# The last two expert positions summed in PSUM instead of through DRAM, with small parameter loads moved from SP to GpSimd

## The chip, the cores and the metric

The kernel runs on one core of a Trainium2 chip. The metric is the device time of one execution in microseconds (us). The engines have separate instruction streams and meet at semaphores: PE (TensorE, matrix products), DVE (VectorE), ACT (ScalarE), POOL (GpSimd) and SP (SyncE, which here only starts transfers). All numbers are float32. Three timed runs of the kernel before gave 972.03, 973.26 and 973.80 us.

## The reference, cut to what matters

Two layers work on 256 latent and 256 context tokens of width 1024. Layer 0 is a mixer of differential attention and mLSTM, layer 1 a two-dimensional Fourier transform with a linear map, and behind each stands the same kind of grouped mixture of experts. After layer 0's mixer only the 256 latent tokens are still needed. For every token a router picks 2 of 16 experts; the layer's own code is

```
y = jnp.zeros_like(h)
for e in range(N_EXPERTS):
    he = jax.nn.silu(h @ w_gate[e]) * (h @ w_up[e])
    y = y + combine[..., e:e + 1] * (he @ w_down[e])
...
x_l = x_l + mod_l[5] * y_l
```

`combine` holds the two shares of a token and is zero elsewhere. `w_gate` and `w_up` are 1024 x 512 and `w_down` is 512 x 1024, so one expert has 6 MB and one layer 96 MB of weights. A `c`-dependent modulation of shift, scale and gate (`silu(c) @ ada_w + ada_b`, 24 column blocks of 512 over both layers) surrounds every sub-layer.

## The kernel before, in words

**Start.** SP loads the inputs and then a stream of 2 MB blocks into six ring slots (`STREAM`, L454): blocks 0 to 3 of the modulation weights (`ada_w`), the key columns of `w_in`, further blocks. Behind the key columns SP also issues the second part of the constants (L463) and seven little loads (L465 to L471: gate columns, convolution taps, router weights and bias, gate bias, sub-norm gain, lambda vectors), and only then the next block of the stream. PE turns blocks 0 to 3 into rows (L1509) and columns (L1518); DVE and ACT modulate the normed input with them (L982, L644); then PE projects the keys (L1578). DVE sums the later modulation blocks itself (`ada0`, L929), eight instructions a block. The first of these is block 4; PE reduces its sum over partitions at L1555 between two projection items.

**Saved modulation sums.** Blocks 12 to 23 belong to layer 1. DVE sums them into the two halves of `bias`, POOL writes each to DRAM (`save`, L562), and DVE may not refill a half until its save has landed. The last block, 23, goes to an area of its own (`third`), which takes that wait away for it.

**Experts.** Positions 0 to 15 of a layer are worked one after another. The tokens of an expert are cut into units of at most 32 rows; a unit's rows were written to DRAM (`unit_rows`) by POOL and are read back by ACT (`load_x`, L793). For a unit PE does `turn_x` (L1786, transpose), `gate_up` (L1809, 64 products), `turn_he` (L1796) and `down` (L1822, 32 products); ACT applies silu (L814); DVE multiplies (`product`, L1366), copies the transposes (L1348, L1354) and scales the result (`result`, L1361). In the usual order PE does `turn_he` of the unit before, `gate_up` of this one, then `down` of the unit before. Weights of three experts fit in SBUF. SP issues an expert's six 1 MB pieces (L485: gate, up, gate, up, down, down) when PE signals that the buffers are free (`expert_begun`, `expert_closed`).

**Results.** DVE puts a result into one of four places of `ys` and ACT stores it with four transfers to DRAM (`unit_results`, L801). When all are stored, POOL fetches with four indirect transfers (`fetch_results`, L584) for each 128-token tile the two result rows of every token, 512 KB each, 2 MB in all. The fetch waits for the landing of the last store. DVE adds them with their shares (`add_fetched`, L1464, four instructions).

**The last position.** Position 15 (`NE - 1`) does not go through DRAM. Its results stay in place 0 of `ys`, and PE multiplies them with a 0-or-share matrix `late_T` straight into banks 0 to 3, which are idle then (`scatter`, L1877). `late_T` is made by DVE from a row of ranks and shares (`late_rows`, 512 columns), which PE makes with one product of `ones` and a table of diagonals (L1891) at position 13; DVE copies it and clears the four banks (`late_row`, L1338 to L1341). At position 15 PE does the `down` of the unit before ahead of `gate_up`. At the end DVE adds the four banks to `xl` (L1457), and the next norm follows. In layer 0 PE also reduces the saved modulation sums of layer 1 (`sum_mod1`, L1924), which SP reads back at L524; four of them stand between the last `down` and the last `scatter`, and they use copies by ACT (L872), which stand behind a wait of ACT for its last row load. `keep_busy` (L1524) are products without use.

## Time and profile before

| | |
|---|---|
| timed runs | 972.03, 973.26, 973.80 us (median 973.26) |
| the profiled execution: its own time | 973.74 us |
| its span, first to last instruction | 971.9 us |
| busy share of the span | PE 83%, weight load 44%, DVE 41%, ACT 18%, POOL 4% |
| the chain that ended last | PE 38%, DMA 26%, DVE 14%, SP's queue 12%, issue 5%, ACT 3% |
| DMA | 320.36 MB, mean 330 GB/s; SP's queue 74.3%, POOL's 5.9%, ACT's 4.8% |
| mean granted TensorE clock | 0.911 of full speed |

The profiled execution is 1.84 us longer than its span, and lies 0.48 us above the median of the timed runs. A busy share is a mean over stages with different limits; the rows below are from single stages. In a timeline the number in brackets is how long the engine had been idle before the row, and what ended that.

### The profile page before, as it was taken

The page shows a single profiled execution, that of the slowest core. Times are in us where ns is not written, and L with a number is a line of the kernel's source. Part 1 is how long each engine was busy: PE and PEld are TensorE (multiplying, and loading weights), DVE is VectorE, ACT ScalarE, POOL GpSimd, SP SyncE. Part 2 cuts the span into 40 slices and gives each one's busy share as a digit, 9 for nine tenths or more (in the row PEclk, how much of TensorE's full clock was granted, in tenths as well). Part 3 has the DMA queues.
Part 4 walks back from the last instruction along what each step waited for, and adds up shares of the span by engine and source line. Part 5 has one row for each costly group of instructions (what it writes and reads, how often), then busy time and mean ns, then how long its engine had stood idle before and what let it go on. Part 6 is the DMA issues. An engine that isn't in the chain of part 4 may idle for free.

```text
span 971.9 us, 18143 instructions
## 1 busy us (share of the span) xinstructions
PE 801.9 (83%) x6954; PEld 432.2 (44%) x6955; DVE 401.4 (41%) x930; ACT 178.0 (18%) x383; POOL 37.9 (4%) x63
## 2 busy tenths in 40 slices
PE   8899989997979685978567986799869979697674
PEld 3544636444554343544234543374335535354332
DVE  3267879867878841211011230433621111112215
ACT  3222010326630111111001110240211110101002
POOL 0000000120000010000000000100010000000010
PEclk9799999999989797999777998799989988899798
DMA  9899977999505987959999999995669899999991
GB/s 342 292 371 348 335 268 269 330 361 314 197 2 216 379 311 277 366 201 414 415 417 415 371 375 413 372 410 227 247 253 412 349 415 415 416 414 416 414 369 56
DMA packets 102104, 320.36 MB, mean 330 GB/s; under 512 B 12704, under 2 KB 27424, under 8 KB 85536
## 3 DMA queue, kind: packets, MB, share of 16 engines
q1 hardware_dynamic: 78448, 282.84, 74.3%
q0 software_dynamic: 4592, 21.54, 5.9%
q10 hardware_dynamic: 19008, 15.22, 4.8%
q8 instruction: 36, 0.59, 0.2%
q14 instruction: 20, 0.16, 0.0%
HBM read 303.71 MB, written 24.25 MB: 337 GB/s over the span
## 4 chain that ended last, share of the span: by engine, by line
PE 38%; DMA 26%; DVE 14%; SPq 12%; issue 5%; ACT 3%; ACTq 2%; POOL 1%; DVEq 0%; POOLq 0%
DMA raw<-in_w_up 12%; DMA arena<-unit_rows 10%; PE bank L1809 8%; SPq L485 8%; PE bank L1588 7%; PE bank L1822 3%; PE bank L1969 3%; PE bank L1524 2%; DVE arena L929 2%; PE bank L1592 2%; PE bank L1597 1%; PE bank L1578 1%; DMA unit_rows<-arena,row_i 1%; SPq L454 1%; SPq L470 1%
## 5 line engine op out<-in xcount | busy, mean ns | idle before, releaser
L1809 PE MATMUL bank<-raw,arena 128*32 128x256 f32 x3392 | 245.7, 428 | 74.2 <-DMA raw<-in_w_up 41.5
L1809 PEld LDWEIGHTS bank<-raw,arena 128*32 128x32 f32 x3392 | 118.5, 120 | 181.1 <-DMA raw<-in_w_up 58.5
L1366 DVE TENSOR_TENSOR arena<-arena,bank 64x256 f32<-64x256 f32 x53 | 22.5, 425 | 339.0 <-ACT arena L814 339.0
L1822 PE MATMUL bank<-raw,arena 128*32 128x256 f32 x1696 | 111.6, 389 | 2.3 <-DVE arena L1354 2.3
L1822 PEld LDWEIGHTS bank<-raw,arena 128*32 128x32 f32 x1696 | 59.6, 113 | 41.4 <-issue 3.7
L1588 PE MATMUL bank<-ring,arena 128*128 128x512 f32 x160 | 69.9, 594 | 0.0
L814 ACT ACTIVATE arena<-bank 64x256 f32<-64x256 f32 x53 | 19.9, 376 | 246.9 <-PE bank L1809 225.5
L1796 PE MATMUL bank<-consts_sb,arena 64*128 64x64 f32 x212 | 36.1, 292 | 32.6 <-DVE arena L1366 21.2
L929 DVE SCALAR_TENSOR_TENSOR bias<-ring,small,bias 128x512 f32<-128x512 f32 x77 | 57.9, 752 | 2.7
L929 DVE SCALAR_TENSOR_TENSOR arena<-ring,small,arena 128x512 f32<-128x512 f32 x63 | 47.4, 752 | 2.2
L1796 PEld LDWEIGHTS bank<-consts_sb,arena 64*128 64x128 f32 x212 | 28.6, 194 | 44.1 <-DVE arena L1366 24.9
L1588 PEld LDWEIGHTS bank<-ring,arena 128*128 128x128 f32 x160 | 30.2, 190 | 37.7 <-issue 37.7
L1524 PE MATMUL bank<-consts_sb 128*128 128x512 f32 x78 | 42.4, 691 | 0.0
L817 ACT COPY arena<-arena 128x256 f32<-128x256 f32 x53 | 21.4, 405 | 113.3 <-DMA arena<-unit_rows 72.3
L814 ACT ACT_TABLE_LOAD x14 | 18.0, 1283 | 95.1 <-issue 95.1
L1361 DVE TENSOR_TENSOR arena<-bank,arena 128x256 f32<-128x256 f32 x49 | 20.8, 425 | 35.1 <-PE bank L1822 34.4
L1578 PE MATMUL bank<-arena,ring 128*128 128x512 f32 x64 | 29.7, 624 | 1.4 <-DVE arena L982 1.4
L1592 PE MATMUL bank<-arena,ring 128*128 128x512 f32 x64 | 29.5, 621 | 0.0
L1730 PE MATMUL bank<-ring,arena 128*128 128x512 f32 x64 | 28.0, 595 | 0.8 <-ACT arena L755 0.8
L1354 DVE COPY arena<-bank 128x128 f32<-128x128 f32 x53 | 15.4, 291 | 29.6 <-PE bank L1796 22.2
L1969 PE MATMUL bank<-ring,arena 128*128 128x512 f32 x64 | 27.6, 592 | 0.0
L659 ACT ACTIVATE arena<-bank 32x256 f32<-32x256 f32 (+2 forms) x30 | 14.3, 476 | 69.5 <-PE bank L1588 45.6
(259 smaller groups left out, 825.3 us busy)
## 6 DMA issues: line engine op xcount, KB each, us to landing
raw<-in_w_gate SPq DMA_DIRECT2D x64, 1024.0 KB, 19.8
raw<-in_w_up SPq DMA_DIRECT2D x64, 1024.0 KB, 21.7
raw<-in_w_down SPq DMA_DIRECT2D x64, 1024.0 KB, 22.7
ring<-in_ada_w SPq DMA_DIRECT2D x24, 2048.0 KB, 13.3
ring<-in_w_in SPq DMA_DIRECT2D x7, 2048.0 KB, 13.5
unit_results<-arena ACTq DMA_DIRECT2D x228, 32.0 KB, 7.2
arena<-unit_rows ACTq DMA_DIRECT2D x55, 128.0 KB, 6.9
ring<-in_w_out SPq DMA_DIRECT2D x2, 2048.0 KB, 42.8
```

Of the source, the lines that this page charges most:

```text
L485: sp.dma_start(dst, src).then_inc(full[s], 16)
L814: nc.scalar.activation(sg[64:P, :], ps[4][0:64, 0:FW], ACT.Silu).then_inc(E["silu_done"], 1)
L929: ins = nc.vector.scalar_tensor_tensor(acc, w[:, k, :], cc[:, k:k + 1], first if k == 0 else acc, ALU.mult, ALU.add)
L1524: mm(ps[bank][:], ident, K_[:, CONSTS["le"][0]:CONSTS["le"][0] + W], start=True, stop=True)
L1578: ins = mm(bank[:], w[:, k, 256 * b + par:256 * (b + 1):2], hT[:, k, :], start=(k == 0), stop=(k == KD - 1))
L1588: ins = mm(bank[:], hT[:, k, t * P:(t + 1) * P], w[:, k, :], start=(k == 0), stop=(k == KD - 1))
L1592: ins = mm(bank[:], w[:, k, a * HD:(a + 1) * HD], hT[:, k, :], start=(k == 0), stop=(k == KD - 1))
L1730: ins = mm(ps[q][:], mgT[:, k, t * P:(t + 1) * P], slot(s)[:, k, :], start=(k == 0), stop=(k == KD - 1))
L1796: ins = mm(ps[6][:, q * 64:(q + 1) * 64], he[64:P, q * P:(q + 1) * P], ident[64:P, 64:P], start=True, stop=True)
L1809: ins = mm(ps[4][o:o + S, 0:FW], xT[:, i, j * S:(j + 1) * S], w[:, k % 4, h * FW:(h + 1) * FW], start=(k == 0), stop=(k == KD - 1))
L1822: ins = mm(ps[5][j * S:(j + 1) * S, 0:XW], hT_e[:, k % QN, k // QN * S:(k // QN + 1) * S], w[:, k % 2, j * XW:(j + 1) * XW], start=(k == 0 ...
L1969: ins = mm(ps[q][:], FT[:, k, t * P:(t + 1) * P], slot(FNET_AT + hf)[:, k, :], start=(k == 0), stop=(k == KD - 1))
```

## The change

Three things change.

- **Two late positions.** `LATE = NE - 2`: positions 14 and 15 are now both summed by `scatter` into banks 0 to 3 and leave out DRAM. PE makes two rows of ranks and shares (into banks 2 and 3), the second kept in the columns of the constants that held the cosine and sine tables. At each of the two positions PE does the `down` of the unit before first, and at position 15 a `scatter` as well, ahead of `gate_up`. The last result that is stored is now position 13's, and `fetch_results` waits for that one. On DVE both `add_fetched` stand in position 15's first unit, ahead of its `product`.
- **Block 23** of the modulation goes through `bias` like the others; the area `third` and SP's waits for the saves are gone.
- **Little loads.** The seven loads are issued by POOL, once PE has used blocks 0 to 2 (`w_used` at 3), and SP goes straight from the constants to the next block.

```diff
@@ the little loads, on SP @@
                 if n == 4:
-                    sp.wait_ge(bias_zero, 2)
                     sp.dma_start(K_[:, K_PARTS[1]:K_PARTS[2]], consts[:, K_PARTS[1]:K_PARTS[2]]
                                  ).then_inc(consts_in, 16)
-                    sp.dma_start(wgt_s.rearrange("p (k n) -> p k n", k=KD),
-                                 w_in_v[:, :, C_G:C_G + NE]).then_inc(smalls_in, 16)
-                    for dst, src in ((convs, convw), (rw_s[:, :, 0:NE], rw.rearrange("(p k) n -> p k n", k=KD)),
...
@@ and on POOL, ahead of its loop over the modulation blocks @@
+            pool.wait_ge(w_used, 3)
+            pool.dma_start(wgt_s.rearrange("p (k n) -> p k n", k=KD),
+                           w_in_v[:, :, C_G:C_G + NE]).then_inc(smalls_in, 16)
...
+            pool.dma_start(lamrow, lamv.to_broadcast([P, 4 * QK])).then_inc(smalls_in, 16)
@@ the fetch, on POOL @@
                 pool.wait_ge(L[l]["y_stored0"], (NE // 2) * 16 * JN)
-                pool.wait_ge(L[l]["y_stored1"], (NE // 2 + 1) * 16 * JN)
+                pool.wait_ge(L[l]["y_stored1"], (NE // 2) * 16 * JN)
@@ ACT, behind position 13 @@
+                n = act.snap(units, min_val=LATE, max_val=MAX_UNITS)
+                store_y(n, n * S, 0)
+                for i in range(LATE, NE):
+                    n_tok = act.value_load(cnt_i[0:1, i:i + 1], min_val=0, max_val=SEQ)
+                    late_unit()
...
@@ DVE, the waits of ada0 @@
-                    if c >= N_ADA + 2 and c < 2 * N_ADA - 1:
+                    if c >= N_ADA + 2:
                         dve.wait_ge(acc_saved[c % 2], 16 * ((c - N_ADA) // 2))
@@ DVE, late_row @@
-                    link(nc.vector.tensor_copy(late_rows, ps[2][:]))
+                    for e in range(2):
+                        link(nc.vector.tensor_copy(late_rows[e], ps[2 + e][:]))
@@ DVE, positions 14 and 15 @@
+                for e in range(2):
...
+                    turn_back(n - 1)
+                    if e == 0:
+                        result(n - 1, 0, NE // 2 - 1)
+                        dve.wait_ge(E["y_stored1"], (NE // 2) * 16 * JN)
+                    else:
+                        late_result(n - 1)
+                        next_weights(1, True)
+                        add_fetched(l, 0)
+                        add_fetched(l, 1)
+                    product(n)
+                    turned(n + 1)
...
                 turn_back(n - 1)
-                add_fetched(l, 0)
                 late_result(n - 1)
-                add_fetched(l, 1)
@@ PE, positions 14 and 15 @@
+                for e in range(2):
+                    ins = mm(ps[2 + e][:], ones, bias[:, e, :], start=True, stop=True)
+                ins.then_inc(late_in_psum, 1)
...
+                for i in range(LATE, NE):
...
+                    turn_he(n - 1)
+                    down(n - 1, prev)
+                    if i > LATE:
+                        scatter(n - 1, False)
+                    gate_up(n, own, True)
+                    turn_x(n + 1, True)
```

PE at the start of position 14 in layer 1, before; `raw_..` are weight pieces, `x8` is eight products of one kind in a row.

```order
L1887 TENSOR_LOAD cnt_i
L1887 ISA x2
L1796 MATMUL bank<-consts_sb,arena 128x64 x2
L1802 REGISTER_ALU
L1809 MATMUL bank<-raw_61,arena 32x256 x2
L1809 MATMUL bank<-raw_62,arena 32x256 x2
```

PE at the same place after the change.

```order
L1904 TENSOR_LOAD cnt_i
L1904 ISA x2
L1804 MATMUL bank<-consts_sb,arena 128x64 x2
L1830 MATMUL bank<-raw_59,arena 32x256 x8
L1830 MATMUL bank<-raw_60,arena 32x256 x8
L1810 REGISTER_ALU
L1817 MATMUL bank<-raw_61,arena 32x256 x2
L1817 MATMUL bank<-raw_62,arena 32x256 x2
```

The `down` of position 13 (L1830, before L1822) stands ahead of position 14's `gate_up` (L1817, before L1809).

DVE at the end of layer 1's experts, before: the last transpose copy, the four adds of fetched rows (L1464) around the last result (L1430), the adds of the four banks (L1457).

```order
L1354 COPY arena<-bank 128x128
L1464 SCALAR_TENSOR_TENSOR xl<-arena,xl 128x1024
L1464 SCALAR_TENSOR_TENSOR xl<-bias,arena,xl 128x1024
L1430 TENSOR_TENSOR arena<-bank,arena 128x256
L1464 SCALAR_TENSOR_TENSOR xl<-arena,xl 128x1024 x2
L1457 TENSOR_TENSOR xl<-xl,bank 128x256 x8
```

DVE after the change, in the first unit of position 15.

```order
L1353 COPY arena<-bank 128x128
L1419 TENSOR_TENSOR arena<-bank,arena 128x256
L1426 COPY arena<-consts_sb 128x1
L1429 ISA
L1316 SCALAR_TENSOR_TENSOR arena<-consts_sb,arena 128x256
L1431 REGISTER_ALU
L1472 SCALAR_TENSOR_TENSOR xl<-arena,xl 128x1024
L1472 SCALAR_TENSOR_TENSOR xl<-bias,arena,xl 128x1024
L1472 SCALAR_TENSOR_TENSOR xl<-arena,xl 128x1024 x2
L1364 REGISTER_ALU
L1365 TENSOR_TENSOR arena<-arena,bank 64x256
```

The four adds (now L1472) have moved from behind the last unit's transpose to a place ahead of the `product` (L1365) of position 15's first unit.

SP in the start stage, before: the constants (L463), the little loads and the next blocks.

```order
L454 DMA ring<-in_w_in 128x8x512
L463 DMA consts_sb<-in_constants 128x1629
L465 DMA small<-in_w_in 128x8x16
L470 DMA small<-in_conv_w 128x24
L470 DMA small<-in_router_w 128x8x16
L470 DMA small<-in_router_b 128x16
L470 DMA small<-in_gate_b 128x16
L470 DMA arena<-in_subln_g 128x128
L471 DMA arena<-in_lam 128x256
L454 DMA ring<-in_ada_w 128x8x512 x4
```

SP after.

```order
L455 DMA ring<-in_w_in 128x8x512
L463 DMA consts_sb<-in_constants 128x1629
L455 DMA ring<-in_ada_w 128x8x512 x4
L455 DMA ring<-in_w_in 128x8x512
L455 DMA ring<-in_ada_w 128x8x512 x3
```

The seven little loads have left SP's queue, and block 4 follows the constants.

## Rows read from the trace of the kernel before

**Rows 1.** Windows: us, busy of PE, PEld, DVE, ACT, POOL, PEclk, DMA share, GB/s.

```profile
932.00:936.00 4.00, 1.11 (x12) 0.15 (x5) 0.00 (x0) 0.00 (x0) 0.00 (x0) 1.00 1.02 408
```

**Rows 2.** Timeline of PE, end of layer 1: start, length, operation [idle before].

```profile
908.10 1.02 PE L1891 MATMUL bank<-bias,consts_sb 128*128 128x512 f32 x2
...
936.11 3.44 PE L1809 MATMUL bank<-raw,arena 128*32 128x256 f32 x28 [2.10 <-DMA raw<-in_w_up]
...
956.89 1.93 PE L1822 MATMUL bank<-raw,arena 128*32 128x256 f32 x32 [0.41 <-DVE arena L1354]
959.94 1.15 PE L1877 MATMUL bank<-arena 32*128 32x256 f32 x16 [1.12 <-DVE arena L1430]
```

**Rows 3.** Timeline of DVE, end of layer 1.

```profile
909.23 0.68 DVE L1338 COPY late_rows<-bank 128x512 f32<-128x512 f32 x1
...
912.97 0.29 DVE L1354 COPY arena<-bank 128x128 f32<-128x128 f32 x1 [0.25 <-issue]
...
940.00 0.42 DVE L1366 TENSOR_TENSOR arena<-arena,bank 64x256 f32<-64x256 f32 x1 [11.66 <-ACT arena L814]
...
962.44 2.73 DVE L1457 TENSOR_TENSOR xl<-xl,bank 128x256 f32<-128x256 f32 x8
```

**Rows 4.** Timeline of ACT, ends of layer 0 and layer 1.

```profile
609.98 0.39 ACTq L793 DMA_DIRECT2D arena<-unit_rows  x1
...
617.08 0.20 ACT L760 ACTIVATE small<-consts_sb 128x1 f32<-128x1 f32 x1 [5.08 <-DMA arena<-unit_rows]
...
929.60 1.78 ACTq L801 DMA_DIRECT2D unit_results<-arena  x4
```

**Rows 5.** Timeline of POOL, the first fetch of each layer.

```profile
611.06 0.98 POOL L584 DMA_INDIRECT arena<-unit_results,row_i  x1 [248.45 <-DMA unit_results<-arena]
...
939.04 0.98 POOL L584 DMA_INDIRECT arena<-unit_results,row_i  x1 [227.70 <-DMA unit_results<-arena]
```

**Rows 6.** DMA queues from 618 to 625 us: packets, MB, share of 16 engines.

```profile
q0 software_dynamic: 403, 1.45, 52.4%
q1 hardware_dynamic: 605, 1.36, 50.9%
```

**Rows 7.** Timeline of DVE, end of layer 0.

```profile
621.08 1.28 DVE L1464 SCALAR_TENSOR_TENSOR xl<-arena,xl 128x1024 f32<-128x1024 f32 x1 [9.45 <-DMA bias<-unit_results,row_i]
...
625.16 2.60 DVE L1464 SCALAR_TENSOR_TENSOR xl<-arena,xl 128x1024 f32<-128x1024 f32 x2 [1.02 <-DMA arena<-unit_results,row_i]
627.98 2.73 DVE L1457 TENSOR_TENSOR xl<-xl,bank 128x256 f32<-128x256 f32 x8 [0.21 <-DVE xl L1464]
```

**Rows 8.** Timeline of PE, end of layer 0.

```profile
617.90 1.96 PE L1924 MATMUL bank<-arena,consts_sb 128*128 128x512 f32 x4 [0.21 <-ACT arena L872]
624.28 2.09 PE L1877 MATMUL bank<-arena 32*128 32x256 f32 x16 [4.42 <-DVE arena L1430]
626.30 3.38 PE L1524 MATMUL bank<-consts_sb 128*128 128x512 f32 x4
...
635.52 3.73 PE L1942 MATMUL bank<-consts_sb,arena 128*128 128x129 f32 x32
```

**Rows 9.** SP's queue in the start stage: the block behind the little loads.

```profile
41.00 12.41 SPq L454 DMA_DIRECT2D ring<-in_ada_w  x4
```

**Rows 10.** Timeline of PE in the start stage.

```profile
32.32 3.33 PE L1509 MATMUL bank<-ring,arena 128*32 128x512 f32 x16 [0.53 <-DMA ring<-in_ada_w]
...
41.80 15.79 PE L1578 MATMUL bank<-arena,ring 128*128 128x512 f32 x32 [1.35 <-DVE arena L982]
58.18 1.12 PE L1555 MATMUL bank<-arena,consts_sb 128*128 128x512 f32 x2 [0.59 <-DVE arena L929]
```

**Rows 11.** Timeline of DVE: modulation blocks 4, 22 and 23, their first instructions.

```profile
51.86 0.75 DVE L929 SCALAR_TENSOR_TENSOR arena<-ring,small,bias 128x512 f32<-128x512 f32 x1 [4.74 <-issue]
...
309.31 0.75 DVE L929 SCALAR_TENSOR_TENSOR bias<-ring,small,consts_sb 128x512 f32<-128x512 f32 x1 [2.65 <-DMA ada_sums<-bias]
...
315.49 0.75 DVE L929 SCALAR_TENSOR_TENSOR arena<-ring,small,consts_sb 128x512 f32<-128x512 f32 x1
```

More of the change, by code:

```diff
@@ L504, in norm_used @@
                     sp.wait_ge(part_ps, l + 1)
-                    for b in range(2):
-                        sp.wait_ge(acc_saved[b], 16 * (N_ADA // 2))
             def stream_used(s):
@@ L1894, in experts @@
[L1894 to L1910 removed]
+                    n = pe.snap(units, min_val=1, max_val=MAX_UNITS)
@@ new lines, in experts @@
+                    turn_he(n - 1)
+                    down(n - 1, prev)
+                    if i > LATE:
+                        scatter(n - 1, False)
+                    gate_up(n, own, True)
+                    turn_x(n + 1, True)
+                    pe.reg_add(units, units, 1)
+                    with pe.If(n_tok > S):
+                        with pe.Fori(S, n_tok, S):
+                            n = pe.snap(units, min_val=1, max_val=MAX_UNITS)
+                            turn_he(n - 1)
+                            gate_up(n, own, False)
+                            down(n - 1, own)
+                            turn_x(n + 1, False)
+                            scatter(n - 1, False)
+                            pe.reg_add(units, units, 1)
```

140 lines of the change are left out of this document (58 added, 82 removed).

## The prediction

> **What bounds the kernel now.** I read the queue table of the page, then windows of 4 us over the end of each layer's experts, then the timelines of PE, DVE, ACT and POOL there, and last the start. At the end of layer 1's experts the transfers set the pace: from 932 to 936 us the 16 DMA engines are fully busy at 408 GB/s, while PE works 1.11 of 4 us [rows 1]. PE's last 28 products of position 15's first `gate_up` begin at 936.11, after 2.10 us of idle time ended by a piece of `up` weights [rows 2]. DVE had been idle for 11.66 us when it does the `product` behind them at 940.00 [rows 3]. What lies between there and the end is a chain of PE and DVE. So two things count: what lands before that last `up` piece, and what DVE does behind the last `down`.
>
> The fetch of results stands in a different place in the two layers. In layer 1 it begins at 939.04 [rows 5], when the last awaited piece has landed, and other work hides it. In layer 0 it begins at 611.06 [rows 5] and is on the path: DVE gets the first tile at 621.08 and the second at 625.16 [rows 7], and the last `scatter` of PE, at 624.28, has waited 4.42 us for DVE [rows 8].
>
> **When the fetch begins after the change.** It now depends on position 13's last result, made by the `down` that comes first at position 14. That `down` needs DVE's transpose copy, at 912.97 [rows 3], which stands behind `late_row`. The second product of `ones` puts 1.02 us before it (length of L1891, [rows 2]) and the second copy 0.68 us [rows 3]: 914.7. The `down` takes 1.93 us at the full clock [rows 2] and up to twice that at the lower level, then 0.42 for the result: stores begin between 917.4 and 919.3. From the stores at 929.60 [rows 4] to the fetch at 939.04 [rows 5] it takes 9.44 us. So the fetch begins between 926.8 and 928.8 instead of 939.04; I take 928. That is 8 us before the last `up` piece lands, inside the stretch where the engines are full.
>
> **Layer 1, the price.** The fetch is 2.1 MB. At 408 GB/s [rows 1] that is 5.1 us, which the weights behind it lose if it goes entirely ahead of them. When both queues had work in layer 0, from 618 to 625, GpSimd's queue moved 1.45 MB and SP's 1.36 MB [rows 6]: equal shares. The other 0.65 MB went in the first 7 us, at less than half of its share. With that slow start the last `up` piece comes about 3.3 us late (0.65 MB owed at 935, paid back at half rate); with equal shares from the start 4.7 to 5.1. Beside it stands DVE: the four adds now come before the `product`. In layer 0 the tiles came 10.0 and 14.1 us after the first issue [rows 5, 7]. From 928 that gives 942.1, and the two adds of the second tile take 2.60 [rows 7]: 944.7. The `product` goes from 940.00 to 944.7, so +4.7 us; bounds 3.3 (only the weights, slow start) and 6.0 (fetch at 928.8 and half a microsecond worse). Position 14's `scatter` (1.15, [rows 2]), the new weights for `late_T`, four more diagonals and the clearing all fall in the 11.66 us of idle time [rows 3] and cost nothing as long as that wait exists. One stored unit less saves 0.13 MB, 0.3 us, which I leave inside the bounds.
>
> The Trainium skill, in "DMA: Bandwidth & Descriptors", section "Queues, rings and completion order", says that every DMA engine goes round the queues that have work and changes at packet boundaries. Rows 6 agree for their 7 us; the first 7 us of that fetch do not. By the rule alone the weights would be 5.1 us late in place of my 4.7 and each layer's `product` 0.4 later.
>
> **Layer 1, the gain at the end.** The last `down` ends at 956.89 + 1.93 = 958.82 [rows 2]. Now the result follows at once (0.42 and some 0.2 of handovers), then the `scatter` (1.15), and the adds of the banks begin at 960.6 instead of 962.44 [rows 3]: −1.8 us. Layer 1 together: +2.9, bounds +1.5 and +4.2.
>
> **Layer 0.** The same order of work shifts position 15's `product` by the same 4.7 us. Then ACT's last load of rows goes from 609.98 to 614.7. It was awaited until 617.08 [rows 4], 7.1 us, so ACT is free at 621.8 for the copies that the second pair of modulation sums needs; that pair goes from 617.90 to 622.6 and ends at 624.6 (1.96, [rows 8]). So the `scatter` starts at 624.6 in place of 624.28: where DVE waited for the fetch, ACT's row load is late next. What is gained is the clock and DVE. Before, PE had idled 4.42 us and the `scatter` took 2.09 [rows 8], against 1.15 at the end of layer 1 [rows 2]: the lower of the two levels, 1.2 GHz against 2.4. Four products behind it took 3.38 [rows 8], so 1.7 at the full clock. Without the idle time this saves up to 0.94 + 1.69 = 2.6 us, and DVE, whose adds begin at 625.8 instead of 627.98 [rows 7], allows 2.2. The first Fourier product (635.52, [rows 8]) comes 2.2 us earlier, or 0.3 later if the clock stays low. I take −1.5, nearer to the full clock; bounds −3.5 (shift of the `product` only 3.3 us) and +1.0.
>
> **The start.** Block 4 was issued at 41.00 [rows 9], behind the seven little loads; now it follows the constants at once. DVE began it at 51.86 [rows 11] and PE waited 0.59 for its sum before 58.18 [rows 10]; a start of the block 0.6 us earlier is enough to take that away: −0.6. PE has no later wait for transfers that this could shorten. Against it, the little loads now run while block 3 is on its way, and PE waits for that block (0.53 idle before 32.32) and from there in one chain to the first projection at 41.80 [rows 10]. POOL may issue them when PE has used block 2, which comes one 2 MB block (5.1 us at the 408 GB/s of [rows 1]) before block 3, so near 28 by estimate; fetched rows needed some us from issue to full share in layer 0 [rows 6], so at most the last 2.4 us before 32.32 are shared equally: 1.2 us, at least nothing. I take +0.5. Together −0.1, bounds −0.6 and +0.6. DVE needs them only behind its part of the modulation, which releases PE at 41.80 [rows 10], so their landing is hardly a risk.
>
> The skill, same page, section "Issuing engines are not separate DMA queues", says that issuing from another engine saves only sequencer time. No row here shows little loads from GpSimd; by the rule block 3 pays for them, as in my +0.5.
>
> **Block 23.** Block 22 began at 309.31 after waiting 2.65 for block 20's save [rows 11]. The save of 21 is one block later, 6.18 us, so it lands at 315.49, just when block 23 starts [rows 11]. 0 to +0.3; I take +0.1.
>
> **Sum.** +2.9 − 1.5 − 0.1 + 0.1 = +1.4 us. On the profiled execution's own 973.74 (span 971.9 and 1.84 around it) that is 975.1. It stands 0.48 above the median of the runs, so I forecast **974.7 us**, +0.15%. This kernel's measurements tell 0.2%, or 1.95 us, from no change, so this counts as no difference.
>
> **Rivals.** *(a) The weights are not held up.* The fetch finds room or is served last. Then layer 1 gains its 1.8; in layer 0 the `scatter` follows the sums at 620.0 in place of 624.28, −4.3, with the clock up to −6.9; the start −0.6. In all −6.7 to −9.3, about 965.3 us. For it: the slow first 7 us in layer 0. Against: 408 GB/s and full engines [rows 1] leave no room. Chance 0.12.
>
> *(b) DVE gets stuck in front of the `product`: slower.* The four adds stand before it, and PE's `turn_he`, all further units and the end stand behind it. This decides as soon as the second tile lands more than about 14 us after the first issue; from there each microsecond costs one in each layer. The weights' queue is deeper here than in layer 0 before. With 2 us more in each: +1.4 + 4.0 = +5.4, 978.7 us. For it: the second tile needed 14.1 us already beside one other queue. Against: the pieces behind the last `up` piece are few. Chance 0.28.
>
> *(c) A milder collision with the clock kept.* Shift 3.3 us in both layers: layer 1 +1.5, layer 0 −3.5, the start −0.6: −2.6, 970.7 us. Chance 0.15.
>
> *(d) The little loads hold up block 3 by more than 1.2 us* or push the constants behind 41.80, which PE also needs: +1 on the forecast, 975.7. Chance 0.05. That the change doesn't do what it says is not in question: the order of instructions shows the moves.
>
> My forecast keeps 0.40, its own range 972.5 to 976.5. The range that should hold 8 in 10 leaves out (a) and the upper part of (b): 970.0 to 978.0. Faster by over 0.2% (below 971.3) holds (a) and most of (c): 0.26. Slower (above 975.2) holds (b), (d) in part and the upper third of the forecast: 0.37. Within: 0.37.
>
> **What would show it.** In layer 1's trace: the fetch near 928 (before 926.8 or after 929 is wrong); the last awaited `up` piece 3.3 to 5 us later; `product` directly behind the fourth add; no add of fetched rows behind the last `down`, 1.8 us between that and the bank adds. In layer 0: the `scatter` near 624.6 and short (1.15). At the start: no wait before L1555's first use, block 3 up to 1.2 us later. If the last `up` piece lands unshifted, the whole of layer 1's price is wrong, and the time is that of (a).

## The result and the profile after

The changed kernel took **985.06 us** (median of 4 runs, 983.35 to 985.42); the kernel before, on the same chip in the same job, 973.53 us (4 runs). The ratio is 1.0112, 95% interval 1.0086 to 1.0137: slower. The forecast of 974.7 us and its range to 978.0 were both wrong. What happened is rival (b), DVE stuck in front of the `product`, at about twice its price (+11.5 us on the medians where it said +5.4). The profiled execution took 985.42 us.

The page of the changed kernel: the span, and PE's and DVE's busy time.

```profile
span 983.6 us, 18211 instructions
...
PE 809.7 (82%) x6990; PEld 436.0 (44%) x6991; DVE 406.1 (41%) x944; ACT 178.1 (18%) x383; POOL 43.0 (4%) x71
```

The span grew by 11.7 us, while the busy shares are what they were or a point less. The loss is waiting. The windows over the end of layer 1's experts show where, with the columns of [rows 1]:

```profile
940.00:944.00 4.00, 0.26 (x2) 0.02 (x1) 0.74 (x1) 0.72 (x2) 0.00 (x0) 0.86 1.02 410
944.00:948.00 4.00, 0.00 (x0) 0.00 (x0) 1.82 (x2) 0.00 (x0) 0.00 (x0) 0.50 0.70 272
948.00:952.00 4.00, 0.41 (x2) 0.41 (x3) 3.42 (x4) 0.00 (x0) 0.00 (x0) 0.50 0.00 0
```

From 940 to 951 PE does nothing, its granted clock falls to half, and at the end the transfers have run dry too: PE waits for DVE, and DVE for the second tile and then for its own two adds. DVE's timeline there answers [rows 3]:

```profile
917.58 0.29 DVE L1353 COPY arena<-bank 128x128 f32<-128x128 f32 x1 [0.23 <-issue]
...
943.25 1.28 DVE L1472 SCALAR_TENSOR_TENSOR xl<-arena,xl 128x1024 f32<-128x1024 f32 x1 [11.34 <-DMA bias<-unit_results,row_i]
...
948.39 2.60 DVE L1472 SCALAR_TENSOR_TENSOR xl<-arena,xl 128x1024 f32<-128x1024 f32 x2 [2.53 <-DMA arena<-unit_results,row_i]
951.12 0.42 DVE L1365 TENSOR_TENSOR arena<-arena,bank 64x256 f32<-64x256 f32 x1
...
974.12 2.73 DVE L1465 TENSOR_TENSOR xl<-xl,bank 128x256 f32<-128x256 f32 x8 [1.34 <-PE bank L1885]
```

The `product` stands right behind the fourth add at 951.12; before it ran at 940.00. Nothing stands any more between the last result and the bank adds but the `scatter`. PE's timeline answers [rows 2]:

```profile
917.92 3.64 PE L1830 MATMUL bank<-raw,arena 128*32 128x256 f32 x32 [4.31 <-DVE arena L1353]
...
937.97 1.92 PE L1817 MATMUL bank<-raw,arena 128*32 128x256 f32 x28 [2.20 <-DMA raw<-in_w_up]
...
951.59 1.11 PE L1804 MATMUL bank<-consts_sb,arena 64*128 64x64 f32 x4 [11.33 <-DVE arena L1365]
952.64 5.54 PE L1817 MATMUL bank<-raw,arena 128*32 128x256 f32 x64
```

The last `up` piece was there at 937.97, only 1.86 us later than before. PE then stood for 11.33 us, and ran the next 64 products at the half clock, 5.54 us; the same 64 take 3.66 in the further unit behind them. ACT's stores of position 13's result and POOL's first fetches of both layers answer [rows 4, 5]:

```profile
922.30 2.48 ACTq L799 DMA_DIRECT2D unit_results<-arena  x4
```

```profile
598.32 0.97 POOL L574 DMA_INDIRECT arena<-unit_results,row_i  x1 [235.60 <-DMA unit_results<-arena]
...
932.41 0.97 POOL L574 DMA_INDIRECT arena<-unit_results,row_i  x1 [218.92 <-DMA unit_results<-arena]
```

The DMA queues while the fetch (GpSimd's queue, q0) and SP's queue (q1) both had work, packets and MB, answer [rows 6]. First the changed kernel from 937 to 943 us, where SP's queue holds weights, then the kernel before from 616 to 622, where it holds the saved sums and constants:

```profile
q1 hardware_dynamic: 329, 1.25, 52.1%
q0 software_dynamic: 325, 1.20, 50.2%
```

```profile
q0 software_dynamic: 424, 1.55, 65.3%
q1 hardware_dynamic: 431, 0.85, 37.6%
```

In both, the two queues moved equal numbers of packets. SP's packets averaged 3.8 KB beside weights and 2.0 KB in the kernel before, the fetch's 3.7 KB in both, so the fetch got 49% of the bytes of the two queues in the first case and 65% in the second.

The end of layer 0, DVE first and PE behind it, answers [rows 7, 8]:

```profile
610.99 1.28 DVE L1472 SCALAR_TENSOR_TENSOR xl<-arena,xl 128x1024 f32<-128x1024 f32 x1 [9.95 <-DMA bias<-unit_results,row_i]
...
616.33 2.60 DVE L1472 SCALAR_TENSOR_TENSOR xl<-arena,xl 128x1024 f32<-128x1024 f32 x2 [2.73 <-DMA arena<-unit_results,row_i]
619.05 0.42 DVE L1365 TENSOR_TENSOR arena<-arena,bank 64x256 f32<-64x256 f32 x1
...
630.06 2.73 DVE L1465 TENSOR_TENSOR xl<-xl,bank 128x256 f32<-128x256 f32 x8 [4.90 <-PE bank L1885]
```

```profile
608.85 3.33 PE L1817 MATMUL bank<-raw,arena 128*32 128x256 f32 x28 [3.19 <-DMA raw<-in_w_up]
...
621.03 3.64 PE L1830 MATMUL bank<-raw,arena 128*32 128x256 f32 x32 [0.38 <-DVE arena L1353]
624.60 4.23 PE L1935 MATMUL bank<-arena,consts_sb 128*128 128x512 f32 x8
628.76 1.15 PE L1885 MATMUL bank<-arena 32*128 32x256 f32 x16
...
637.66 3.73 PE L1953 MATMUL bank<-consts_sb,arena 128*128 128x129 f32 x32
```

The `product` comes at 619.05 (609.36 before), the last `down` behind it at the half clock, and the first Fourier product at 637.66 where it was at 635.52.

**The loss, added up.** POOL wrote layer 1's rows at 708.11, 2.15 us later than before (705.96): that is layer 0 and the start. From there to layer 1's `product` it takes 8.97 us more (951.12 − 708.11 against 940.00 − 705.96). Behind the `product`, 64 + 4 products at the half clock cost 1.88 + 0.45 = 2.33, and the order at the end gives 1.77 back. Together 2.15 + 8.97 + 0.56 = 11.68 of 11.7 us.

### The profile page after: what moved, and what is told of

Its sections match the earlier page's. It is cut to its first block, busy times and chain, and to the rows that moved or that the text cites. A ratio compares the mean times of both kernels' runs of the same rounds, so it can differ in the third digit from the quotient of the medians.

```text
span 983.6 us, 18211 instructions
## 1 busy us (share of the span) xinstructions
PE 809.7 (82%) x6990; PEld 436.0 (44%) x6991; DVE 406.1 (41%) x944; ACT 178.1 (18%) x383; POOL 43.0 (4%) x71
## 4 chain that ended last, share of the span: by engine, by line
PE 45%; DMA 23%; DVE 14%; SPq 8%; issue 5%; ACT 2%; ACTq 2%; POOL 1%; DVEq 0%; POOLq 0%
PE bank L1817 10%; DMA raw<-in_w_up 10%; PE bank L1596 7%; PE bank L1830 6%; DMA arena<-unit_rows 6%; SPq L478 5%; PE bank L1586 3%; PE bank L1980 3%; DMA arena<-unit_results,row_i 3%; PE bank L1600 2%; DMA consts_sb<-in_constants 2%; PE bank L1532 2%; DVE bias L925 2%; PE bank L1804 1%; PE bank L1605 1%
## 5 line engine op out<-in xcount | busy, mean ns | idle before, releaser
L1817 PE MATMUL bank<-raw,arena 128*32 128x256 f32 x3392 | 244.4, 430 | 65.8 <-DMA raw<-in_w_up 36.0
L1817 PEld LDWEIGHTS bank<-raw,arena 128*32 128x32 f32 x3392 | 119.0, 121 | 172.7 <-DMA raw<-in_w_up 51.0
L1365 DVE TENSOR_TENSOR arena<-arena,bank 64x256 f32<-64x256 f32 x53 | 22.5, 425 | 304.8 <-ACT arena L812 299.9
L1830 PE MATMUL bank<-raw,arena 128*32 128x256 f32 x1696 | 114.8, 401 | 10.2 <-DVE arena L1353 10.2
L1830 PEld LDWEIGHTS bank<-raw,arena 128*32 128x32 f32 x1696 | 59.7, 116 | 51.5 <-DVE arena L1353 11.1
L925 DVE SCALAR_TENSOR_TENSOR bias<-ring,small,bias 128x512 f32<-128x512 f32 x84 | 63.2, 752 | 3.0
L925 DVE SCALAR_TENSOR_TENSOR arena<-ring,small,arena 128x512 f32<-128x512 f32 x56 | 42.1, 752 | 2.0
L1532 PE MATMUL bank<-consts_sb 128*128 128x512 f32 x78 | 38.9, 642 | 0.0
L1600 PE MATMUL bank<-arena,ring 128*128 128x512 f32 x64 | 28.5, 605 | 0.0
L1353 DVE COPY arena<-bank 128x128 f32<-128x128 f32 x53 | 15.4, 291 | 28.5 <-PE bank L1804 20.7
```

The source lines that it names most:

```text
L925: ins = nc.vector.scalar_tensor_tensor(acc, w[:, k, :], cc[:, k:k + 1], first if k == 0 else acc, ALU.mult, ALU.add)
L1532: mm(ps[bank][:], ident, K_[:, CONSTS["le"][0]:CONSTS["le"][0] + W], start=True, stop=True)
L1600: ins = mm(bank[:], w[:, k, a * HD:(a + 1) * HD], hT[:, k, :], start=(k == 0), stop=(k == KD - 1))
L1817: ins = mm(ps[4][o:o + S, 0:FW], xT[:, i, j * S:(j + 1) * S], w[:, k % 4, h * FW:(h + 1) * FW], start=(k == 0), stop=(k == KD - 1))
L1830: ins = mm(ps[5][j * S:(j + 1) * S, 0:XW], hT_e[:, k % QN, k // QN * S:(k // QN + 1) * S], w[:, k % 2, j * XW:(j + 1) * XW], start=(k == 0 ...
```

## The experiments

One table serves them all. It gives four stretches of each profiled execution in us: from POOL's first write of rows (L564 of the changed kernel) to the start of the last awaited `up` piece's products, in each layer, then from there to the first Fourier product (layer 0) and to the bank adds (layer 1). What lies between Fourier and layer 1's rows took 70.4 to 70.5 us in all but one (71.5), and what follows the bank adds 9.5 to 9.6. "Early" says where the fetch is released: behind position 13's result (early) or later.

| kernel | fetch | rows to last up, layer 0 | last up to Fourier | rows to last up, layer 1 | last up to bank adds | median us | ratio to before |
|---|---|---|---|---|---|---|---|
| before | late | 249.2 | 28.5 | 230.2 | 26.3 | 973.53 | 1 |
| changed | early | 251.0 | 28.8 | 229.9 | 36.2 | 985.06 | 1.0112 |
| e1 | early | 252.0 | 26.6 | 230.5 | 26.3 | 974.39 | 1.0007 |
| e2 | late | 247.9 | 28.6 | 230.1 | 26.5 | 972.19 | 0.9990 |
| e3 | early | 251.0 | 28.2 | 230.7 | 29.8 | 978.58 | 1.0061 |
| e4 | early | 250.9 | 26.3 | 230.7 | 34.3 | 983.08 | 1.0119 |
| e5 | early | 251.2 | 25.2 | 230.4 | 25.8 | 971.94 | 0.9966 |
| e6 | late | 249.2 | 29.0 | 229.0 | 28.7 | 974.40 | 0.9990 |
| e7 | late | 248.6 | 28.7 | 229.4 | 27.3 | 972.41 | 0.9986 |
| e8 | early | 250.0 | 24.6 | 230.6 | 30.9 | 976.01 | 1.0004 |
| e9 | early | 249.9 | 27.2 | 229.3 | 25.8 | 970.63 | 0.9969 |
| e10 | early | 253.0 | 27.5 | 231.1 | 35.5 | 980.24 | 1.0064 |

The kernel before ran beside each: 973.31 us for e1 to e4, 974.69 for e5 to e8, 973.58 for e9 and e10. Intervals stand with each experiment.

**e1_adds_last: the changed kernel with the adds where they were.**

```diff
@@ changed kernel, DVE, position 15 @@
                         next_weights(1, True)
-                        add_fetched(l, 0)
-                        add_fetched(l, 1)
@@ behind the last copy of transposes @@
                 turn_back(n - 1)
+                add_fetched(l, 0)
                 late_result(n - 1)
+                add_fetched(l, 1)
```

> The kernel after, with the four adds of fetched rows put back behind the last unit's transpose copy (tile 0 before the last result, tile 1 behind it), as the kernel before has them. All else stays: both late positions, down first, the early fetch, block 23, little loads by GpSimd. Theory O (order): DVE waits for the second tile ahead of position 15's product, and that wait is the loss. Then the product of layer 1 comes back from 951.1 to about 942.3 (940.0 plus the 2.2 us by which the stage starts later), PE does not drop to the lower clock there (-2.3), the 1.8 us gained at the end are lost again: -9.5 in layer 1 and -2 to -4 in layer 0, 972 to 975 us. Theory B (bandwidth): the early fetch takes the time from the weights, wherever DVE uses it: 982 us or more.

974.39 us (12 runs), ratio 1.0007, 0.9988 to 1.0025: the whole loss is gone. PE and then DVE at the end of layer 1:

```profile
938.26 3.39 PE L1817 MATMUL bank<-raw,arena 128*32 128x256 f32 x28 [2.98 <-DMA raw<-in_w_up]
```

```profile
942.11 0.42 DVE L1365 TENSOR_TENSOR arena<-arena,bank 64x256 f32<-64x256 f32 x1 [11.59 <-ACT arena L812]
...
961.86 2.60 DVE L1472 SCALAR_TENSOR_TENSOR xl<-arena,xl 128x1024 f32<-128x1024 f32 x2
964.58 2.84 DVE L1465 TENSOR_TENSOR xl<-xl,bank 128x256 f32<-128x256 f32 x8
```

The `product` follows the weights again, although the fetch is as early as in the changed kernel (930.38). So the early fetch, the second late position, the `down` first and the little loads together cost nothing that can be measured; the place of the adds costs it all.

**e2_little_loads: the kernel before with only the little loads moved to POOL.**

```diff
@@ kernel before, SP @@
-                    sp.wait_ge(bias_zero, 2)
...
-                    sp.dma_start(lamrow, lamv.to_broadcast([P, 4 * QK])).then_inc(smalls_in, 16)
@@ POOL, ahead of its loop over the modulation blocks @@
+            pool.wait_ge(w_used, 3)
...
+            pool.dma_start(lamrow, lamv.to_broadcast([P, 4 * QK])).then_inc(smalls_in, 16)
```

> The kernel before with one part of the change alone: the seven little loads issued by GpSimd once PE has used block 2, and SP going straight on. Theory O: this part costs nearly nothing at the end: PE starts the keys up to 1 us late, part of which is made up by a higher clock, 973.3 to 974.8 us. Rival S (start): the little loads and the extra queue cost 3 us or more in all, 976.5 us or more.

972.19 us (12 runs), ratio 0.9990, 0.9973 to 1.0007: no difference, under the 973.3 that was the lower end expected. PE in the start stage:

```profile
42.37 16.27 PE L1578 MATMUL bank<-arena,ring 128*128 128x512 f32 x32 [2.71 <-DMA consts_sb<-in_constants]
58.48 1.02 PE L1555 MATMUL bank<-arena,consts_sb 128*128 128x512 f32 x2
```

The keys now wait for the constants (42.37 against 41.80), and the wait of 0.59 before L1555 is gone, as forecast; L1555 itself comes 0.30 later.

**e3_adds_one_step_later: the adds behind position 15's `product`, ahead of the copy of the transposes.**

```diff
@@ changed kernel, DVE, position 15 @@
-                        add_fetched(l, 0)
-                        add_fetched(l, 1)
                     product(n)
                     turned(n + 1)
+                    if e == 1:
+                        add_fetched(l, 0)
+                        add_fetched(l, 1)
```

> The kernel after, with the four adds one step further down in DVE's stream: behind product and the copy of the next rows in position 15's first unit, still ahead of that unit's transpose copy. Theory O gives a dose: in layer 1 PE can now do the whole second gate_up before it needs DVE, so the wait of DVE for the second tile (until about 951) holds up PE by some 4.5 us instead of 9, and PE hardly drops its clock; in layer 0, with one unit, hardly more than 2 us come back. 975 to 979 us. Theory B: no difference to the kernel after, 983 to 986 us.

978.58 us (7 runs), ratio 1.0061, 1.0041 to 1.0081. DVE in layer 1:

```profile
947.85 2.61 DVE L1473 SCALAR_TENSOR_TENSOR xl<-arena,xl 128x1024 f32<-128x1024 f32 x2 [1.47 <-DMA arena<-unit_results,row_i]
950.82 0.29 DVE L1353 COPY arena<-bank 128x128 f32<-128x128 f32 x1 [0.36 <-DVE xl L1473]
```

The same tile is waited for, but PE has the 64 products of the next unit to do meanwhile and lacks only the copy: half of the loss. Here the wait cost what stood behind it in the order, not what it lasted.

**e4_pe_kept_busy: the changed kernel with 7 (layer 0) and 12 (layer 1) calls of `keep_busy`, of two products each, for PE while DVE waits behind position 15's first `gate_up`.**

```diff
@@ changed kernel, PE, positions 14 and 15, ahead of turn_he @@
+                    if i > LATE:
+                        keep_busy((7, 12)[l], 5)
```

> The kernel after, with products without use (7 in layer 0, 12 in layer 1, into a bank that is free) while PE waits for DVE behind position 15's first gate_up. Theory O counts 11.1 us for DVE's wait in layer 1 and a further 2.3 us because PE restarts at the lower clock (the 64 products behind the wait take 5.5 instead of 3.7 us, the four before them 1.1 instead of 0.66). Then this kernel gets back 2.3 us in layer 1 and 0 to 2 in layer 0: 981 to 983 us. If the lower clock isn't due to the idle time, nothing comes back: 984.5 to 986 us.

983.08 us (4 runs), ratio 1.0119, 1.0084 to 1.0155; by the time it can't be told from the changed kernel, so neither expectation is confirmed by it. The trace shows the clock's share:

```profile
939.62 10.46 PE L1532 MATMUL bank<-consts_sb 128*128 128x512 f32 x24
950.01 0.66 PE L1804 MATMUL bank<-consts_sb,arena 64*128 64x64 f32 x4
950.60 3.66 PE L1817 MATMUL bank<-raw,arena 128*32 128x256 f32 x64
```

With work in the gap the 64 products take 3.66 us and the four 0.66: 2.33 saved behind the wait. The useless products ran 1.8 us past DVE's `product` at 947.78 and ate most of it; in layer 0, where they ended in time, the stretch to Fourier shrank from 28.8 to 26.3. The Trainium skill, "TensorE: Matmul & The Clock Gate", Part 1 on the clock gate, says that the gate sets the array's clock by how busy PE has recently been; these rows agree. Behind the wait the lower clock costs 2.3 us in layer 1 and about as much in layer 0; it is a follow-up cost, not the cause. How long DVE's wait is doesn't set it: the same 64 products took 6.02 us in e10 behind 6.99 us without work, 6.10 in e8 behind 4.21, and 5.25 to 5.6 in e5, e7 and e9 behind 0.31. PE also stands still for the weights before them, and in the kernel before the lower clock fell on the 28 products ahead of the `product` instead (3.44 us, 1.92 in the changed kernel).

**e5_adds_in_idle: tile 0's adds behind position 15's own unit, tile 1's behind its first further unit.**

```diff
@@ e1, DVE, position 15 @@
+                        add_fetched(l, 0)
                         with dve.If(n_tok > S):
+                            further_unit()
+                            add_fetched(l, 1)
...
                 turn_back(n - 1)
-                add_fetched(l, 0)
                 late_result(n - 1)
-                add_fetched(l, 1)
+                with dve.If(n_tok <= S):
+                    add_fetched(l, 1)
```

> The changed kernel with the four adds moved into VectorE's idle time: tile 0's two behind position 15's own unit, tile 1's two behind its first further unit (behind the last product where it has none). Nothing is left out. With the adds behind the last transpose copy, as in e1_adds_last, the bank adds of layer 1 began at 964.58 because the fourth add ended at 964.46, while the product they need could have been scattered at about 961.5. Theory O (the changed kernel lost its time only because VectorE waited for tile 1 ahead of position 15's product; every wait of 3.7 us between two further units holds two adds of 2.6 us for nothing): bank adds about 1.8 us earlier, so 971.8 to 973.4 us. Rival (the adds delay the transposes' copies and with them the down products, or tile 1 is not there when its place comes): 974.5 or more.

971.94 us (12 runs), ratio **0.9966, 0.9947 to 0.9984**: faster than the kernel before. In layer 1 tile 0 was 1.92 us late for its place, which hid behind PE's 64 products. In layer 0 it was there in time, but its adds held the copy for the last `down`, which waited 3.46 us and ran at the half clock (3.64); the stretch to Fourier, which goes over the modulation sums, was 25.2 us all the same. The profiled execution (975.67 us) was the slowest of the twelve and wrote layer 0's first rows 3.5 us later than the kernel before's (361.31 against 357.78); why isn't known.

**e6_fetch_behind_weights: e1, but ScalarE releases the fetch only behind position 15's own unit.**

```diff
@@ e1, ACT @@
-                nc.scalar.copy(s_done[:, l:l + 1], ident[:, 0:1]).then_inc(further_stored, 1)
...
                     late_unit()
+                    if i > LATE:
+                        nc.scalar.copy(s_done[:, l:l + 1], ident[:, 0:1]).then_inc(further_stored, 1)
```

> As e1_adds_last (adds behind the last transpose copy), and the fetch released by ScalarE only behind position 15's own unit, when all weights of the layer have landed. Nothing is left out. Measured so far: from position 14's last `up` piece to position 15's is 5.62 and 5.54 us in the kernel before (layers 0 and 1), 6.73 and 6.08 in e1_adds_last. Theory F (the early fetch holds these weights up): the steps go back to 5.5 to 5.7 us in both layers. Theory P (the down-first order at position 14 frees weight buffers later): the steps stay at 6.1 to 6.7. For the time: layer 1 gains at most 0.5, layer 0 wins 1.2 on the weights and loses about as much on tiles that land at 629, so 973 to 976 us either way; a sum above 978 would say that the fetch's earlier place carries more than I think.

974.40 us (10 runs), ratio 0.9990, 0.9972 to 1.0008, inside what both expected. The step between the last two `up` pieces tells them apart; PE at the end of layer 0:

```profile
601.05 1.92 PE L1818 MATMUL bank<-raw,arena 128*32 128x256 f32 x28 [1.96 <-DMA raw<-in_w_up]
...
606.39 2.43 PE L1818 MATMUL bank<-raw,arena 128*32 128x256 f32 x28 [2.23 <-DMA raw<-in_w_up]
```

5.34 us here and 4.99 in layer 1, against 6.73 and 6.08 in e1 and 5.62 and 5.54 before. In layer 0 theory F holds: this step took 6.1 to 7.2 us in the eight kernels with an early fetch and 5.3 to 5.6 in the four with a late one, and from the rows to the last `up` piece the early ones took 249.9 to 253.0 us, the late ones 247.9 to 249.2. In layer 1 single executions don't settle it: where the rows show the step, it was 5.47 (the changed kernel itself) to 6.08 with an early fetch and 4.99 to 5.60 with a late one.

**e7_before_adds_in_idle: the kernel before with e2's little loads and the adds in the further units' idle time.**

```diff
@@ kernel before, DVE, position 15's further units and the end @@
+                    further_unit()
+                    add_fetched(l, 0)
...
                 turn_back(n - 1)
-                add_fetched(l, 0)
+                with dve.If(n_tok > S):
+                    add_fetched(l, 1)
...
+                with dve.If(n_tok <= S):
+                    add_fetched(l, 0)
                 late_result(n - 1)
-                add_fetched(l, 1)
+                with dve.If(n_tok <= S):
+                    add_fetched(l, 1)
```

> The kernel before with the little loads issued by GpSimd (as e2_little_loads) and, in a layer where the last expert has further units, tile 0's adds behind its first further unit and tile 1's ahead of the last product instead of behind it. Nothing is left out. In the kernel before layer 1's bank adds began at 962.44 behind the fourth add; the products they need were scattered from 959.94 on, which lets them begin at about 961.2. Theory O: 1.2 us less than e2_little_loads (972.2), so 970.4 to 971.6 us, under the kernel before. Rival (tile 0 lands after its place, as tile 1 did in the changed kernel, and holds the copy for the second further unit's down products): no gain or a loss, 972 to 975.

972.41 us (12 runs), ratio 0.9986, 0.9971 to 1.0001: not the 1.2 us less than e2. In its trace the fourth add delays the last result by about half a microsecond, and the 64 products of the first further unit ran at the half clock, 5.6 us. With a late fetch there is one idle place fewer in which a landed tile can be added.

**e8_second_tile_last: the changed kernel with only tile 1's adds moved to the end.**

```diff
@@ changed kernel, DVE @@
                         add_fetched(l, 0)
-                        add_fetched(l, 1)
...
                 late_result(n - 1)
+                add_fetched(l, 1)
```

> The changed kernel with only tile 0's two adds ahead of position 15's product; tile 1's two go behind the last product. Nothing is left out. In the changed kernel tile 0's adds ended at 945.85, tile 1's at 950.99, and the product ran at 951.12. Theory O: the product runs at about 946.1, 5.0 us earlier, PE stands still shorter, and tile 1's adds come back to the end for 0 to 1.8 us: 978.5 to 982 us, between e1_adds_last (974.4) and the changed kernel (985.1). Rival (the price is not the place of the wait but something else that the adds' early place does, such as writes to xl beside the matmuls): 983 or more.

976.01 us (10 runs), ratio 1.0004, 0.9984 to 1.0023: below the range expected. DVE in layer 1, and PE in layer 0:

```profile
936.98 1.28 DVE L1472 SCALAR_TENSOR_TENSOR xl<-arena,xl 128x1024 f32<-128x1024 f32 x1 [9.23 <-DMA bias<-unit_results,row_i]
...
939.71 0.42 DVE L1365 TENSOR_TENSOR arena<-arena,bank 64x256 f32<-64x256 f32 x1
```

```profile
608.08 3.45 PE L1817 MATMUL bank<-raw,arena 128*32 128x256 f32 x28 [3.15 <-DMA raw<-in_w_up]
...
615.04 3.74 PE L1830 MATMUL bank<-raw,arena 128*32 128x256 f32 x32 [0.38 <-DVE arena L1353]
619.97 3.85 PE L1935 MATMUL bank<-arena,consts_sb 128*128 128x512 f32 x8 [1.19 <-DMA arena<-ada_sums]
...
632.65 3.73 PE L1953 MATMUL bank<-consts_sb,arena 128*128 128x129 f32 x32
```

In layer 1 the `product` comes 13.97 us after the fetch's first issue (925.74) instead of 18.71, 4.7 us earlier where 5.0 were expected, and the stretch from the last `up` piece to the bank adds is 5.3 us shorter (30.9 against 36.2). What the expectation left out is layer 0: without the wait for tile 1 the last `down` starts at 615.04 instead of 621.03, and Fourier comes 24.6 us after the last `up` piece instead of 28.8. So, by these single executions, tile 1's wait and adds cost 4.2 us in layer 0 and 5.3 in layer 1.

**e9_adds_behind_copies: as e5, each pair of adds behind the copy of the transposes.**

```diff
@@ e1, DVE, position 15 @@
+                    def further_unit(t=None):
...
+                        turn_back(n - 1)
+                        if t is not None:
+                            add_fetched(l, t)
+                        product(n)
...
+                        with dve.If(n_tok > S):
+                            further_unit(0)
+                            with dve.If(n_tok > 2 * S):
+                                further_unit(1)
...
-                add_fetched(l, 0)
+                with dve.If(n_tok <= S):
+                    add_fetched(l, 0)
                 late_result(n - 1)
-                add_fetched(l, 1)
+                with dve.If(n_tok <= 2 * S):
+                    add_fetched(l, 1)
```

> As e5_adds_in_idle, but each pair of adds stands behind the copy of the transposed activations instead of ahead of it: tile 0's in the first further unit, tile 1's in the second, both at their former place behind the last product where a layer has no further unit (layer 0). Nothing is left out. In e5_adds_in_idle VectorE waited 1.92 us for tile 0 in layer 1, and the copy behind it ran at 947.26, 4.7 us after it could have; in layer 0 the copy ran at 620.49 and the down products started at 620.84 at the half clock. Theory O: the copies no longer wait, layer 1's bank adds come at most 0.8 us earlier relative to the last weights, layer 0 is as in e1_adds_last or up to 1.4 us longer: 970.5 to 973 us, under the kernel before (974). Rival (the code that is written out a second time, or tile 0 landing behind the first product's due time, costs): 974 or more.

970.63 us (12 runs), ratio **0.9969, 0.9947 to 0.9991**: with e5 the fastest, and not told from it. DVE in layer 1, and PE's 64 products of the first further unit:

```profile
939.04 1.28 DVE L1491 SCALAR_TENSOR_TENSOR xl<-arena,xl 128x1024 f32<-128x1024 f32 x1
...
944.48 0.42 DVE L1365 TENSOR_TENSOR arena<-arena,bank 64x256 f32<-64x256 f32 x1 [2.83 <-ACT arena L812]
...
948.35 2.60 DVE L1491 SCALAR_TENSOR_TENSOR xl<-arena,xl 128x1024 f32<-128x1024 f32 x2
952.15 0.42 DVE L1365 TENSOR_TENSOR arena<-arena,bank 64x256 f32<-64x256 f32 x1 [1.20 <-ACT arena L812]
```

```profile
938.61 5.38 PE L1836 MATMUL bank<-raw,arena 128*32 128x256 f32 x64
```

All four adds lie before a wait of DVE for ACT that is still there behind them (2.83 and 1.20 us left): in layer 1 they cost nothing. The traces don't place the whole gain. This profiled execution is 2.5 us shorter than the kernel before's, and only 0.5 of that lies at layer 1's end (25.8 against 26.3): the order there gives 1.77 back, but behind the last `up` piece the lower clock fell on the 64 products (5.38 us) instead of the 28, which costs 1.24. The rest lies in stretches where single executions of kernels with the same structure differ by as much.

**e10_wait_alone: e1 with only the two waits ahead of position 15's `product`.**

```diff
@@ e1, DVE, position 15 @@
                         next_weights(1, True)
+                        for t in range(TT):
+                            dve.wait_ge(y_back[t], 32 * (l + 1))
```

> e1_adds_last with VectorE's wait for both fetched tiles put back ahead of position 15's product, and the four adds left behind the last product. Nothing is left out. Theory O (it is the wait for tile 1's landing, with the arithmetic worth only the 2.6 us that stand behind it): position 15's product runs 2.7 us earlier than in the changed kernel, relative to the fetch's first issue, and the end pays up to 1.8 us for the adds: from the last `up` piece to layer 1's bank adds about 35 us (36.15 in the changed kernel, 26.32 in e1_adds_last), 983 to 985 us. Rival (the arithmetic itself, 5.2 us on VectorE, is the price): near e1_adds_last, under 979.

980.24 us (10 runs), ratio 1.0064, 1.0045 to 1.0083: between the two expectations. DVE's `product`:

```profile
950.15 0.42 DVE L1365 TENSOR_TENSOR arena<-arena,bank 64x256 f32<-64x256 f32 x1 [15.44 <-DMA arena<-unit_results,row_i]
```

That is 15.55 us after the fetch's first issue (934.60); in the changed kernel it was 18.71, so the arithmetic ahead of the `product` adds 3.2 us to the wait. The stretch to the bank adds, 35.5, is what theory O said, but this profiled execution (986.73 us) was the slowest of the ten and the rest lie between 978.99 and 982.81. By the ratios the wait alone carries about half of the loss (0.0057 over e1, of 0.0105), so theory O is right that the wait costs by itself, and its size is open; why the other nine were some 6 us faster than the profiled one isn't known, as they have no trace.

## Why the prediction was wrong, step by step

- **What bounds it, and the moves**: right. Before and after, the end of a layer is a chain of weights, then PE and DVE, and the forecast named the instruction that would be late.
- **Layer 1, the price: the step that failed.** It said the `product` moves by +4.7 us; it moved by +11.1. Its sum was 928 + 14.1 + 2.60 = 944.7; measured were 932.41 + 15.98 + 2.60, and 0.13 of handover, 951.12. The fetch's begin was 4.4 too early and the landing 1.9 too short. *The fetch's begin* was 932.41, not 928: 2.15 us came from the stretch before; the copy for position 13's `down` came 0.7 later than that (917.58); that `down` ran at the half clock (3.64 us, the slow end that I had named, while I took a value inside the range), some 0.9; and from the stores (922.30) to the fetch it took 10.1, not 9.44. *The landing*: tile 0 was added 10.8 and tile 1 16.0 us after the first issue, where I carried over the 10.0 and 14.1 of [rows 5, 7]; in layer 0 it was 12.7 and 18.0, and with e6's late fetch 9.7 and 13.6 again. The slow start was right, and the same in both kernels: beside a working SP queue no packet of the fetch moved in its first 4 us. What failed is the reading of [rows 6] as equal shares. Those 7 us run past the end of the fetch; from 616 to 622 it had 1.55 MB against 0.85, for equal packets (424 and 431). Beside the weights' larger packets (325 and 329, 1.20 and 1.25 MB) its rate fell from 0.26 to 0.20 MB a microsecond. That the packet sizes are the reason is argued from these rows; no run changed them alone. The upper bound of +4.2 for the layer allowed half a microsecond for this, while the rival's own argument (2 us more) was the likelier size.
- **The half clock behind the wait** was nowhere in layer 1's sum: 2.33 us behind the `product`. I had used the same effect in layer 0 as a gain.
- **The weights held up by 3.3 to 5.1 us**: wrong in size. They came 1.8 us late in layer 0 and −0.3 in layer 1 (230.2 to 229.9). In layer 1 the last awaited `up` piece was there 5.6 us after the first issue (937.97), when the fetch had moved 0.29 MB, worth 0.7 us at the 410 GB/s of that stretch; in layer 0 it was there 10.5 us after, and the fetch had moved 1.04 MB, worth 2.5. The forecast put 8 us between the two in layer 1. From the fourth microsecond on the queues took turns packet by packet, as the rule of the Trainium skill that the forecast weighed ("DMA: Bandwidth & Descriptors", "Queues, rings and completion order") says; the 5.1 us late weights that the forecast drew from it need equal shares from the first issue on, and no run shows that.
- **The gain at the end, −1.8**: right, 1.77 in the changed kernel; e5 and e9 keep it.
- **Layer 0, −1.5**: wrong, it became +2.1, nearly all between its rows and Fourier (+1.8 up to the last `up` piece, +0.3 behind it). The `product` came at 619.05, not 614.1, again from tile 1. The chain that I had named behind it (sums, then `scatter`) was right, and the `scatter` took 1.15 at the full clock; but the `down` ahead of it fell to the half clock and started 5 us late. e8 shows the 4.2 us that tile 1's wait costs here.
- **The start and block 23**: right within their bounds. L1563 now begins at 59.24 without a wait (58.18 before), because the keys wait for the constants (42.34), and in e2 this cost nothing by the time. Block 23 (316.70) follows block 22 (310.52) in the same 6.18 us as before. Both parts together: POOL's first write of layer 0's rows is at 357.86, before at 357.78.

PE of the changed kernel at the start, for [rows 10]:

```profile
42.34 17.07 PE L1586 MATMUL bank<-arena,ring 128*128 128x512 f32 x32 [1.55 <-DMA consts_sb<-in_constants]
59.24 1.02 PE L1563 MATMUL bank<-arena,consts_sb 128*128 128x512 f32 x2
```

Rival (b) had the place and the rule ("each microsecond costs one"), and "the pieces behind the last `up` piece are few" was the wrong reason against it: the two `down` pieces of 1 MB stand there, and from 937.97 until tile 1 was there (948.39) SP's queue moved 1.61 MB beside the fetch's 1.81. It should have been the forecast. What stays open is the split of layer 0's early part between the fetch and chance (single profiled executions of kernels with the same structure differ by 1 to 3 us there), and e10's distance from its trace.

## What to carry to other kernels

Before work that waits for a transfer is moved up in an engine's order, look at what stands behind it on that engine: where another engine needs that work, the wait costs in full, and the matrix engine that stands still behind it may restart at the slower clock. Add a landed tile where the engine has an idle gap that another wait ends, and late enough that the transfer needn't be counted on to the microsecond; the same four adds cost 10 us ahead of the `product` and nothing at the end, and with them in the gaps the kernel was 3 us (0.3%) faster than the one before. A transfer's time read beside one kind of traffic can't be carried over to another: compare packets and bytes of both queues first.

## What the runs showed of the hardware

- Four indirect fetches of 512 KB each by GpSimd were used 9.7 to 10.1 us (first tile) and 13.6 to 14.2 us (second) after the first issue beside the sums and constants in SP's queue, and 10.8 to 12.7 and 15.5 to 18.0 us beside the weights.
- Beside a working SP queue the first packet of such a fetch moved between 4.0 and 4.5 us after the first issue (both layers of the changed kernel, layer 0 before); in layer 1 before, with 0.3 MB left in SP's queue, it moved within 2 us.
- From then on the two queues moved equal numbers of packets (325 to 329, 424 to 431), and bytes by their packets' size (1.20 to 1.25 MB, 1.55 to 0.85).
- After 11.3 us without work PE ran 64 products in 5.54 us instead of 3.66; with 24 useless products in the gap, in 3.66. After 0.31 us, behind waits for weights, they took 5.38 in e9.
- In e6 the last 32 `down` products of layer 1's first further unit took 4.4 us instead of 1.9 at a full granted clock, while the fetch (issued from 940.33 to 945.05) ran. No row shows what they waited for, and the cause is open:

```profile
943.16 1.13 PE L1831 MATMUL bank<-raw,arena 128*32 128x256 f32 x6
944.62 0.64 PE L1831 MATMUL bank<-raw,arena 128*32 128x256 f32 x4 [0.33 <-issue]
946.03 1.53 PE L1831 MATMUL bank<-raw,arena 128*32 128x256 f32 x22 [0.78 <-issue]
```
